# A hybrid conv/mLSTM decoder layer: the mixer's front rebuilt (prefix state as X^T diag(w) K times W_v)

## The reference

```python
proj = h @ w_in        # gb, gc, u (1024 each) | q, k (512 each) | v, o (1024 each) | i, f (4 each)
y_conv = gb * causal_dwconv3(gc * u, short_conv_w)
...
# mLSTM, 4 heads, dk = 128, dv = 256: C_t = f_t C_{t-1} + i_t v_t k_t^T ; n_t = f_t n_{t-1} + i_t k_t
# h_t = (C_t q_t) / max(|n_t . q_t|, 1), then a per-head RMSNorm and the sigmoid gate of o
...
x = x + concat(y_conv, y_m) @ w_out
x = x + (silu(g) * u) @ w_down,  [g, u] = causal_dwconv3(rmsnorm(x) @ w_up) + b
x = x + sigmoid(rmsnorm(x) @ w_pg) * (p @ w_pp)
out = rmsnorm(x)
```

## Time and profile before

| | |
|---|---|
| median of 6 runs | 1764.16 us (1760.87 to 1862.26) |
| the profiled execution's own time | 1761.47 us |
| its span, slowest core (core 0) | 1759.9 us |
| spans of the 8 cores | 1749.7 to 1759.9 us |
| mean granted TensorE clock of the cores | 0.985 to 0.990 of full speed |
| PE busy | 1661.6 us, 94% of the span, 11268 matmuls |
| DVE, ACT, POOL busy | 738.1, 390.8, 71.6 us |
| HBM read | 295.77 MB |

### The profile page before, as it was taken

One profiled execution on the slowest core, in us unless ns is written; L12 is line 12 of the kernel. 1 busy time (PEld: TensorE's weight loads), 2 busy tenths in 40 slices (PEclk: granted clock), 3 DMA queues, 4 the chain that ended last, 5 costly groups with the idle time before them and its releaser, 6 DMA issues.

```text
span 1759.9 us, 27766 instructions; the slowest of 8 cores (1749.7 to 1759.9 us)
## 1 busy us (share of the span) xinstructions
PE 1661.6 (94%) x11268; PEld 1072.0 (61%) x11310; DVE 738.1 (42%) x1123; ACT 390.8 (22%) x583; POOL 71.6 (4%) x138
## 2 busy tenths in 40 slices
PE   1999999989988999999999999999999999999995
PEld 1888868856655666666654466666445666544442
DVE  3543301233444466444431134444311444465756
ACT  3230032222332222222210022222000222222232
POOL 0000000000000000000000000000000000000000
PEclk9999999999999999999999999999999999999997
DMA  9944424424336937444444444444444444449884
GB/s 259 240 100 73 73 49 73 73 49 73 60 61 181 192 60 120 72 73 78 81 80 74 72 72 75 78 80 80 73 72 72 76 81 72 85 74 170 147 158 157
DMA packets 26733, 171.13 MB, mean 97 GB/s; under 512 B 3184, under 2 KB 3184, under 8 KB 9456
## 3 DMA queue, kind: packets, MB, share of 16 engines
q0 software_dynamic: 19552, 134.82, 45.6%
q1 hardware_dynamic: 7056, 34.55, 5.9%
HBM read 295.77 MB, written 8.39 MB: 173 GB/s over the span
## 4 chain that ended last, share of the span: by engine, by line
PE 88%; DVE 4%; ACT 2%; issue 2%; DMA 2%; DVEq 0%; ACTq 0%; POOL 0%; SPq 0%; POOLq 0%
PE psB L518 32%; PE psA L518 24%; PE psB L504 9%; PE psA L504 4%; PE psA L869 3%; PE psB L869 3%; PE psA L1141 3%; PE psA L1046 2%; PE psB L1046 2%; PE psB L1141 1%; DMA arena<-xsl 1%; DVE arena L1176 1%; DMA wsl<-w_down_b 1%; PE psC L413 1%; ACT regE L662 0%
## 5 line engine op out<-in xcount | busy, mean ns | idle before, releaser
L518 PE MATMUL psB<-hT,wsl 128*128 128x344 bf16 (+2 forms) x3312 | 501.1, 312 | 8.7 <-DVE yT L739 8.7
L518 PEld LDWEIGHTS psB<-hT,wsl 128*128 128x128 bf16 x3312 | 324.4, 98 | 172.6 <-issue 9.5
L518 PE MATMUL psA<-hT,wsl 128*128 128x344 bf16 (+1 forms) x2160 | 327.7, 312 | 2.1 <-DVE regE L968 2.1
L518 PEld LDWEIGHTS psA<-hT,wsl 128*128 128x128 bf16 x2160 | 212.2, 98 | 110.5 <-issue 3.3
L964 ACT ACTIVATE regE<-psA,cst_sb 128x1026 f32<-128x1026 f32 x44 | 53.1, 1207 | 394.3 <-PE psA L518 385.7
L504 PE MATMUL psB<-wsl,hT 128*128 128x256 bf16 x1152 | 130.0, 275 | 0.0
L966 DVE SCALAR_TENSOR_TENSOR regE<-psA,cst_sb,regE 128x1026 f32<-128x1026 f32 x44 | 56.6, 1286 | 165.0 <-ACT regE L964 165.0
L504 PEld LDWEIGHTS psB<-wsl,hT 128*128 128x128 bf16 x1152 | 113.5, 99 | 14.2
L966 DVE SCALAR_TENSOR_TENSOR regE<-psB,cst_sb,regE 128x1026 f32<-128x1026 f32 x44 | 56.6, 1286 | 154.6 <-ACT regE L964 154.6
L518 PE MATMUL psB<-yT,wsl 128*128 128x512 bf16 x502 | 112.6, 378 | 0.5
L518 PE MATMUL psA<-yT,wsl 128*128 128x512 bf16 x500 | 112.2, 378 | 0.6
(11 more groups left out here) (172 smaller groups left out, 1532.7 us busy)
## 6 DMA issues: line engine op xcount, KB each, us to landing
wsl<-w_up_b POOLq DMA_DIRECT2D x44, 1024.0 KB, 8.7
wsl<-w_in_b POOLq DMA_DIRECT2D x30, 1024.0 KB, 8.6
wsl<-w_down_b POOLq DMA_DIRECT2D x16, 1024.0 KB, 8.5
wsl<-w_pg_b POOLq DMA_DIRECT2D x16, 1024.0 KB, 9.8
wsl<-w_out_b POOLq DMA_DIRECT2D x10, 1024.0 KB, 9.5
wsl<-w_down_b POOLq DMA_DIRECT2D x12, 768.0 KB, 8.5
arena<-xr SPq DMA_DIRECT2D x4, 2058.0 KB, 19.8
arena<-xsl SPq DMA_DIRECT2D x8, 1024.0 KB, 11.0
```

The lines of the kernel that those rows point to most:

```text
L518: P.op("pe", lambda e, k=k, si=si, c0=c0, w=w: e.matmul(ps[:, si, 0:w], lhsT=slot[:, k, j * 128:(j + 1) * 128], rhs=src[:, k, c0:c0 + w], ...
```

## The change

1. **Prefix state.** v of the prefix is no longer computed. With w_t the decay and input weight of token t (from suffix sums of the log gates) and r_t its rstd, the state of a head is (X^T diag(w r^2) K) W_v: `state_m` forms M = X^T (w K) for 16 feature blocks, 7 matmuls of 512 columns each, and `v_task` multiplies M by the same W_v block that the main tokens use. K of the prefix comes from x without its rstd.
2. **Opening.** The prefix x is streamed by feature blocks, with the matching block of w_k, both cast on POOL's queue (`prefix_load`); each block's matmuls accumulate into seven PSUM banks (`prefix_step`). The prefix x is loaded a second time, token-major (`load_x_tm`), for `state_m`. The main slabs become nine of 128 tokens, which go through the weight slots in f32; k is made over 512 columns at once, a tile behind the slab.
3. **q and o.** Both over the 1026 tokens that are needed, in slices of 342; o feature-major, with the gain as a per-partition scalar; the o gate is applied on DVE after the transposes.
4. **Chunks.** Scores of chunk T+1 are emitted right after the outputs of chunk T; denominators come before numerators; `ym` is a scaled copy on ACT; the row scale and the clearing of the sums go to POOL. The convolution is a stream of 72 slices of 16 matmuls with buffers per slice, 3 before and 5 after each state update.
5. **Tiles.** A tile knows its address range; the first write to it waits for live tiles that overlap it (`claim`), and the hand-made lists go, among them those of `ple_loads`. The left margin of x shrinks from 5 to 2 columns.

```diff
+    def claim(self, w):
+        if w.rng is None or w.live:
+            return
+        keep = []
+        for r in self.live:
+            if r.rng[0] == w.rng[0] and r.rng[1] < w.rng[2] and w.rng[1] < r.rng[2]:
+                self.alias(w, [r])
+                r.live = False
...
-                if j < NS and wstate.get("gate") is not None:
-                    g = wstate["gate"]
-                    g.signal = True
-                    o.deps.append(g)
...
+    def prefix_load(k):
+        P.op("pool", lambda e: e.dma_start(out=Wk[:, k, :], in_=w_k[k]), writes=[RWk[k]], dma=True)
+        P.op("pool", lambda e: e.dma_start(out=xT_p[:, k, :], in_=xp_k[k]), writes=[RxTp[k]], dma=True)
...
+    def prefix_step(k):
+        P.op("act", lambda e: e.activation(out=sq_p[k % 2], in_=xT_p[:, k, :], func=AF.Square), reads=[RxTp[k]], writes=[Rsq_p[k % 2]])
+        if k < 15:
+            prefix_scale(k)
+        for t in range(7):
+            ps, Rp = kp_banks[t]
+            P.op("pe", lambda e, t=t, ps=ps: e.matmul(ps[:, 0:512], lhsT=xT_p[:, k, 128 * t:128 * (t + 1)], rhs=Wkg[:, k, :],
+                                                      start=(k == 0), stop=(k == 15)), reads=[RxTp[k], RWkg[k]], writes=[Rp])
...
+    def load_x_tm():
+        for t in range(7):
+            P.op("pool", lambda e, t=t: e.dma_start(out=x_tm[:, t, :], in_=xp_t[t]), writes=[Rx_tm[t]], dma=True)
+
+    def state_m():
+        for f in range(16):
+            ps, Rp = next_bank()
+            for t in range(7):
+                P.op("pe", lambda e, t=t, f=f, ps=ps: e.matmul(ps[:, 0:512], lhsT=x_tm[:, t, 128 * f:128 * (f + 1)], rhs=wk[:, t, :],
+                                                               start=(t == 0), stop=(t == 6)), reads=[Rx_tm[t], Rwk[t]], writes=[Rp])
...
+            ps, Rp = next_bank()
+            for k in range(16):
+                P.op("pe", lambda e, k=k, ps=ps: e.matmul(ps[:, 0:256], lhsT=M[:, k, 128 * h:128 * (h + 1)], rhs=slot[:, k, 0:256],
+                                                          start=(k == 0), stop=(k == 15)), reads=[RM[k], Rs], writes=[Rp])
...
+        P.op("pool", lambda e: e.tensor_tensor(out=S["rowsc"], in0=S["cc"], in1=S["rr"], op=ALU.mult), reads=[Rsm["cc"], Rsm["rr"]], writes=[Rsm["rowsc"]])
...
-                out=ym[:, h * 256:(h + 1) * 256], in0=pn, scalar=rowsc[:, h:h + 1], in1=og[:, T, h * 256:(h + 1) * 256],
...
+            P.op("act", lambda e, h=h, pn=pn: e.activation(out=ym[:, h * 256:(h + 1) * 256], in_=pn, func=AF.Copy, scale=S["rowsc"][:, h:h + 1]),
...
+    call(setup)
+    for k in range(1, 12):
+        call(lambda k=k: prefix_load(k))
+    prefetch(1)
+    for k in range(12, 16):
+        call(lambda k=k: prefix_load(k))
+    prefetch(4)
+    for k in range(14):
+        call(lambda k=k: prefix_step(k))
...
+        if s == 7:
+            call(load_x_tm)
+    call(lambda: k_tile(8))
+    call(lambda: [gate_tile(t) for t in range(9)])
+    call(lambda: (gates_main(), q_zero()))
+    call(lambda: [weigh_keys(t) for t in range(7)])
+    q_task(0)
+    call(gates_main_weights)
+    q_task(1)
+    call(state_m)
     for h in range(4):
...
+        v_task(h)
     for b in range(4):
...
+        if b == 3:
+            call(lambda: mlstm_scores(0))
+        o_task(b)
+    stream = conv_stream()
     for T in range(9):
...
+        call(lambda T=T: mlstm_out(T))
         if T < 8:
...
+            call(lambda T=T: mlstm_scores(T + 1))
+        for _ in range(3):
+            next(stream)
+        if T < 8:
+            call(lambda T=T: mlstm_update(T))
+        call(lambda T=T: mlstm_gate_out(T))
+        for _ in range(5):
+            next(stream, None)
...
     def ple_loads():
-        P.alias(Rppw, RaT)
-        P.alias(RpTb, Rupg + Rupu)
...
+    Y_ORDER = list(range(6)) + list(range(8, 16)) + [6, 7]
```

More of the change, by code:

```diff
@@ L57, in op @@
         deps = []
+        for r in reads:
+            assert r.rng is None or r.live, r.name
+        for w in writes:
+            self.claim(w)
         for r in reads:
@@ L229, in build_nc @@
[L229 to L248, removed]
@@ L274, in build_nc @@
+    Sm, RSm = [], []
+    for i in range(2):
+        v, r = small_bf("Sm%d" % i, 512)
+        Sm.append(v.rearrange("p (h n) -> p h n", h=4)); RSm.append(r)
+    ym, Rym = small_bf("ym", 1024)
+    junk, Rjunk = small("junk", 256)
     class GateSet:
@@ new lines, in norm_square, with norm_stat @@
+    def norm_square(s, sl, Rs):
+        for g in range(4):
+            P.op("act", lambda e, g=g: e.activation(out=sqd[s % 2][:, 4 * g:4 * (g + 1), :], in_=sl[:, 4 * g:4 * (g + 1), :], func=AF.Square),
+                 reads=[Rs], writes=[Rsqd[s % 2][g]])
+    def norm_stat(s, ps, Rp, shared=False):
+        for k in range(16):
+            fl = dict(start=False, stop=False, skip_group_check=True) if shared else dict(start=(k == 0), stop=(k == 15))
+            P.op("pe", lambda e, k=k, fl=fl: e.matmul(ps, lhsT=ones_bf, rhs=sqd[s % 2][:, k, :], **fl),
+                 reads=[Rsqd[s % 2][k // 4], Rcbf], writes=[Rp])
@@ L604, in q_task, with q_zero @@
+    own_slices = [(126 + 342 * s, 342) for s in range(3)]
+    own_src = lambda k, si: hT_reads(k, *own_slices[si])
+    def q_zero():
+        for h in range(4):
+            P.op("dve", lambda e, h=h: e.memset(qT[:, h, 0:126], 0.0), writes=[RqT[h]])
     def q_task(j):
@@ new lines, in o_task, with consume @@
+    def o_task(b):
+        def consume(slot, Rs):
+            for jj in range(2):
+                j = 2 * b + jj
+                ps, Rb = feat_major_proj(slot, Rs, jj, hT, None, 16, own_slices, own_src)
+                P.op("act", lambda e, ps=ps, j=j: e.activation(out=oT[:, j, :].rearrange("p (s n) -> p s n", s=3), in_=ps[:, :, 0:342], func=AF.Sigmoid),
+                     reads=Rb, writes=[RoT[j]])
+                P.op("dve", lambda e, j=j: e.tensor_scalar(out=oT[:, j, :], in0=oT[:, j, :], scalar1=cs(C_GMH + j), scalar2=None, op0=ALU.mult),
+                     reads=[RoT[j], Rcst], writes=[RoT[j]])
+        return task(blk(w_in_b, 20 + b), 16, 256, consume)
@@ new lines, in conv_stream @@
+    def conv_stream():
+        for b in range(4):
+            for kind, c in (("gc", 4), ("u", 8), ("gb", 0)):
+                at = None
+                for j in range(2):
+                    for si in range(3):
+                        fn = conv_slice(kind, b, j, si)
+                        if at is None:
+                            at = task(blk(w_in_b, c + b), 16, 256, fn)
+                        else:
+                            again(at, fn)
+                        yield
+    call(setup)
@@ new lines, in slab_norm, with consume, after_first @@
+    def slab_norm(s, then):
+        def consume(slot, Rs):
+            ps, Rp = psS[0] if s == 0 else psS[1]
+            norm_stat(s, ps, Rp, shared=(s == 0))
+            if s == 0:
+                prefix_scale(15)
+            norm_rstd(s, ps, Rp)
+            norm_apply(s, slot, Rs)
+            then()
+        again(slab_at[s], consume)
+    def after_first():
+        prefix_step(15)
+        prefix_stat(15)
+        late.append(k_tile(0))
+    late = []
+    slab_task(0)
+    call(lambda: prefix_step(14))
```

872 lines of the change are left out of this document (399 added, 473 removed).

## The result

The changed kernel took **1668.3 us** (median of 10 runs, 1666.85 to 1752.01) beside 1762.8 us of the kernel before: a ratio of **0.9451**, 95% interval 0.9421 to 0.9481. On another chip it was 0.9474 (0.9460 to 0.9488). Single executions far above the rest, such as 1752 us, are those in which the cores of one die ran at a lower granted clock than the others; the ratios leave them out. The forecast, 1670 against 1764.16, is a ratio of 0.9466.

What follows compares the result with a forecast made beforehand. PE's busy time bounds the kernel nearly everywhere, DMA the opening. w_out starting at 473.2 instead of 560.2 (minus 87.0) and tail minus 7.1 make 94 off the 1764.16 us median: 1670, range 1654 to 1704.

Steps and rivals of the forecast that it cites:

- the front: Everything before w_out: w_out was to start at 473.2 instead of 560.2 us, minus 87.0.
- those on the masked scores, on w_pp and on w_down: Signs: no PE wait on masked scores or w_down; POOL's w_pp load right behind a w_down load, not 28 us after.
- Opening: Prefix loads: DMA sets the pace for 13.1 MB, last block landing at 43 us, upper bound 51.
- Main slabs and gates: Last block to q: 46.3 us of PE work plus 5.7 of waits (bounds 0 and 13), 52.
- q, state, v, o: Stages from q to o, priced by matmul columns: 31.3, 25.0, 72.2 and 56.1 us, ending at 279.6.
- Convolution and chunks: Stage before w_out: 168.6 us convolution, 21 chunk matmuls, 4 waits (bounds 0 and 20), 193.6; about 1 us cover left.
- rival (a): Chunk stage: chain not covered, nine chunks each wait some 2 us and the clock may fall; plus 20, 1690; chance 0.15.
- Tail: End of the FFN: w_pp's load no longer holds back w_down reloads; wait and slow matmuls go, minus 7.1 us.
- (b): Opening: blocks don't overlap, each pays 2.0 us fixed cost; plus 32, 1702 us; chance 0.10.
- (d): Tail: the address-range dependences don't release the w_pp load's tile; 1677 us; chance 0.05.
- (e): Opening: each block pays a 9.9 us landing in a full queue; plus 117, 1787 us, slower; chance 0.03.
- (c): Opening: PE, fed block by block, stays at 1.2 GHz, 3.6 us per step; plus 15, 1685 us; chance 0.07.

Runs made afterwards that it cites:

- one slice less: Changed kernel with two convolution slices instead of three between a chunk's output and its state update, six behind it: 1690.4 us, ratio 0.9571.
- the two tail runs: Changed kernel with the w_pp load again waiting for all of aT: ratio 0.9498; kernel before with that load waiting only for the four overwritten tiles: 0.9953.
- the pairs: Changed kernel with the sixteen prefix feature blocks loaded in pairs, eight transfers each of x and w_k, same bytes: 1670.9 us, ratio 0.9461.

## Why the prediction was right, and where it was not

The time was right to 2 us and so was the mechanism. Part of the closeness is luck: the front was 4.8 us better in the forecast than measured (87.0 against 82.2), and behind w_out the kernel gained 11.1 us instead of 7.1. Of the signs it named, those on the masked scores, on w_pp and on w_down held; three times came late, the last block's step at 48.3 us (46), q at 102.9 (95) and w_out at 478.0 (473).

- **Opening: a term mis-sized.** "DMA sets the pace" held. The term is the landing of the last block: 47.0 us (issued at 38.25, 8.8 to landing, core 4) and not 43. The steady rate was not the fault: 325 GB/s lies within the 312 to 348 of the earlier trace rows. Two things were missing: the first 8 us, at some 255 GB/s, and the next main slabs, whose loads go out from 38.94 us and share the queue with the last block (0.6 MB by its landing, by the trace's packet records). Block 12 came at 39.9 and PE needs 7.2 us from there to slab 0's statistics (47.35), so what was to begin at 43 began at 47.4. The bounds held this: the small casting load gave 51.
- **Main slabs and gates: a term mis-sized.** From the first statistics to q 55.5 us instead of 52. Waits: 2.4 for ACT's squares, 1.0 for the suffix sums, 0.2, and the stop of 3.8, which the prediction did not have here. It had seen one such stop, 4.33 us in the earlier trace rows, and left it open for the opening alone; 144 tiny matmuls in a row were in its sum only with their 3.9 us of work. Spreading them took the stop away, so it is not their work; but the row alone does not make it either, for the 144 of the kernel before at 133.40 ran through in 3.86 us (the last section has what the stop waits for).
- **q, state, v, o** took 30.9, 24.7, 73.5 and 56.0 us against 31.3, 25.0, 72.2 and 56.1. Counting columns was enough, and the run with the old state confirms it with 20.0 against 20.7. The slow start of q, 2.3 forecast, was 2.7.
- **Convolution and chunks** took 190.0 instead of 193.6. The chain was covered, and the price of rival (a), 20 us, was right: one slice less cost about that. But the slack was less than "about 1 us": 0.3 in the second chunk, since the chain from the first DVE step to the end of the copies is 7.2 us there, not 6.6. From the end of the rsqrt to the first copy it is 0.5 us (0.3 assumed): POOL's product takes 0.20, the hand-overs 0.2 ahead of it and 0.1 behind. The four copies take 2.17, not 1.71.
- **Tail.** Minus 7.1 forecast; 87.1 to 79.4 is minus 7.7, and the two tail runs gave 7.1 and 9.0.
- **The rest behind w_out**, 3.4 us, was not foreseen. 1.7 of it is the first group of the FFN, 7.17 us instead of 8.86; five of the changed kernel's cores show 8.85 there, and why three don't is open. The other 1.7 us were not traced.
- **Rivals.** (b) falls with the last block's landing at 47.0 and not 75, and with the pairs, (d) with the tail runs, (e) with landings that overlap. Of (c) a piece came true: the first two steps and block 12's, after its wait, ran at 3.2 instead of 1.86 us.

## What to carry to other kernels

When a load stage is bound by bytes, price it with its slow start and with everything that shares its queue; here pairing or reordering the transfers moved the stop and did not shorten the stage. Weave tiny matmuls between long ones: here in a row they cost more than their work, each time in the clock of what followed and mostly in a stop as well. Where a chain is "just covered", look for its slack in the trace: past it every chunk waits, and the waits can cost clock as well.

## What was not expected of the hardware

A run of 113 matmuls of 8 columns ended, on every core, in a stop of 0.8 to 3.8 us without a releaser, and the granted clock behind it was 0.50 for some 7 us even where the stop was 0.8. In the other runs that keep the row together the stop stands behind the 107th to the 116th matmul and is 0.2 to 3.7 us long, and on three cores there is none. In groups of 16 and 32 neither stop nor low clock appeared. DMA queues of the whole span, and of the stretch 98 to 102 us on core 4, which is the stop (queue, kind: packets, MB, share):

```profile
q8 instruction: 86, 1.41, 0.3%
```

```profile
q0 software_dynamic: 79, 0.64, 103.0%
q8 instruction: 1, 0.02, 1.5%
```

The instruction queue moved 1.41 MB in 86 packets, 16 KB each, and one of them lies in the stop, on engines that x_tm's loads keep full. The Trainium skill, Runtime: NRT & Kernel Launch, section "Instruction fetch mechanics", says that instructions come in blocks of 16 KiB, 256 instructions, over a DMA queue of the engine's own, mostly hidden; 113 matmuls with their weight loads are 226. Packet size and place agree with a block that came late, and the trace's records of single DMA packets bear it out (us):

| | instruction packet ends | matmuls go on | stop |
|---|---|---|---|
| changed kernel, core 0 | 97.15 | 98.58 | 0.83 |
| changed kernel, core 4 | 100.43 | 101.86 | 3.81 |
| one slice less, core 6 | 97.72 | 98.95 (the 114th, worked out) | none |

In the nine profiles that keep the row together, 69 of 72 cores stop, and PE goes on 1.0 to 1.7 us after the packet's end, however long the stop. So it is with the 4.33 us stop of the kernel before: 1.3 to 1.5 us after a packet on all eight cores. In that kernel's row at 133.40, which no core interrupts, the packet had ended 3.1 to 3.7 us before the row began. So what PE waits for is an instruction packet; the times show it, no run that moves the packet. Why it is late is open: tiny matmuls use instructions up fast, and x_tm's loads fill the queues; a run without those loads there was not made.

Nor was it expected that the read rate of the opening, some 325 GB/s from 10 to 38 us, would hardly move with the size of the pieces (2%) or the number in flight.
